# Moving the preparation transposes of a hybrid decoder kernel: both groups behind the up unit

## What is computed

```python
def swiglu_ffn(h, w_in, w_out):
    gate, up = jnp.split(h @ w_in, 2, axis=-1)
    return (jax.nn.silu(gate) * up) @ w_out

# S5, per group of 16 channels a 64-dimensional complex diagonal state
b_bar = ((lam_bar - 1.0) / lam)[:, :, None] * lax.complex(b_re, b_im)
bu = jnp.einsum('gph,btgh->btgp', b_bar, u_blk)
_, s = lax.associative_scan(_linear_recurrence_op, (a_elems, bu), axis=1)
y_blk = jnp.einsum('ghp,btgp->btgh', c, s).real
```

## Time and profile before

| | |
|---|---|
| median of 3 runs | 1010.5 us (1010.32 to 1010.53) |
| the profiled execution | 1009.69 us |
| its span | 1008.0 us |
| busy PE, DVE, ACT, POOL | 98%, 73%, 56%, 11% of the span |
| mean granted clock of PE | 0.998 |
| turns 7 to 21 in the span | 69.0 us to 212 us |

### The profile page before, as it was taken

How to read it: one execution, slowest core, us unless ns; L and a number is a source line. 1 busy time by engine, 2 the same in 40 slices (tenths; PEclk the granted TensorE clock), 3 DMA queues, 4 the chain that set the end, 5 groups by cost and what they waited for, 6 DMA issues and landing times.

```text
span 1008.0 us, 20116 instructions
## 1 busy us (share of the span) xinstructions
PE 990.0 (98%) x7672; PEld 923.4 (92%) x7672; DVE 738.5 (73%) x900; ACT 567.3 (56%) x790; POOL 111.6 (11%) x143
## 2 busy tenths in 40 slices
PE   8999999899899999999999999999999999999997
PEld 8999999899899999999999999999899898888886
DVE  5789885799976766666687666668566587666666
ACT  7444446583365655555565555555599765555555
POOL 4863138000001000000010000001000010000000
PEclk9999999999999999999999999999999999999999
DMA  8655554343065555555546556554643246556552
GB/s 253 191 181 173 172 173 159 130 151 119 23 210 188 173 193 182 187 185 188 185 147 210 187 187 187 187 187 148 219 137 127 84 147 211 192 192 189 189 188 110
DMA packets 49037, 172.42 MB, mean 171 GB/s; under 512 B 6096, under 2 KB 6096, under 8 KB 48976
## 3 DMA queue, kind: packets, MB, share of 16 engines
q1 hardware_dynamic: 48544, 170.99, 51.9%
q10 hardware_dynamic: 432, 0.55, 0.2%
HBM read 170.47 MB, written 1.05 MB: 170 GB/s over the span
## 4 chain that ended last, share of the span: by engine, by line
PE 74%; DVE 12%; POOL 6%; issue 4%; ACT 3%; DMA 1%; ACTq 0%; DVEq 0%; POOLq 0%; SPq 0%
PE mx L1195 11%; PE gu L1195 10%; PE mx L1198 6%; PE gu L1198 5%; PE gu L1180 5%; PE gu L1181 5%; PE gu L1182 5%; PE acc L1180 5%; PE acc L1181 5%; PE acc L1182 5%; DVE w_lo L732 3%; PE acc L1224 2%; PE acc L1226 2%; PE acc L1228 2%; ACT w_hi L334 1%
## 5 line engine op out<-in xcount | busy, mean ns | idle before, releaser
L804 DVE TENSOR_TENSOR w_lo<-raw,w_hi 128x1024 fp32r<-128x1024 f32 x178 | 217.2, 1222 | 56.2 <-ACT w_hi L419 55.2
L732 DVE TENSOR_TENSOR w_lo<-raw,w_hi 128x1024 fp32r<-128x1024 f32 x138 | 177.0, 1297 | 41.6 <-ACT w_hi L334 41.0
L419 ACT ACTIVATE w_hi<-raw 128x1024 fp32r<-128x1024 f32 x171 | 179.8, 1053 | 41.3 <-PE mx L1198 18.3
L1180 PE MATMUL gu<-g,w_hi 128*128 128x256 f32 x624 | 179.6, 288 | 1.9 <-DVE g L824 1.6
L1181 PE MATMUL gu<-g,w_hi 128*128 128x256 f32 x624 | 176.5, 283 | 0.0
L1182 PE MATMUL gu<-g,w_lo 128*128 128x256 f32 x624 | 176.4, 283 | 0.0
L334 ACT ACTIVATE w_hi<-raw 128x1024 fp32r<-128x1024 f32 x145 | 150.2, 1051 | 41.1 <-DMA raw<-wstream_dram 20.4
L1180 PE MATMUL acc<-h_hi,w_hi 128*128 128x256 f32 x504 | 143.6, 285 | 0.1
L1182 PE MATMUL acc<-h_hi,w_lo 128*128 128x256 f32 x504 | 142.6, 283 | 0.0
L1181 PE MATMUL acc<-h_lo,w_hi 128*128 128x256 f32 x504 | 142.6, 283 | 0.0
L1180 PEld LDWEIGHTS gu<-g,w_hi 128*128 128x128 f32 x624 | 119.5, 192 | 2.9 <-DVE w_lo L1099 2.1
(11 more groups left out here) (280 smaller groups left out, 1691.0 us busy)
## 6 DMA issues: line engine op xcount, KB each, us to landing
raw<-wstream_dram SPq DMA_DIRECT2D x318, 512.0 KB, 3.6
x<-x_in_dram SPq DMA_DIRECT2D x4, 256.0 KB, 5.7
raw<-wstream_dram SPq DMA_DIRECT2D x3, 256.0 KB, 5.7
out_dram<-x_tok SPq DMA_DIRECT2D x3, 256.0 KB, 2.0
gain_row<-last_gain_dram SPq DMA_DIRECT2D x1, 512.0 KB, 4.7
raw<-wstream_dram ACTq DMA_DIRECT2D x1, 256.0 KB, 4.3
s_memory<-b_re_dram SPq DMA_DIRECT2D x1, 256.0 KB, 4.5
s_memory<-b_im_dram SPq DMA_DIRECT2D x1, 256.0 KB, 4.6
```

Source lines behind the costliest of these rows:

```text
L419: act.activation(w_hi[:, n0 % RING, :], raw[:, n0 % RAW, :], ACT.Copy).then_inc(hi_ready, 1)
L732: dve.tensor_tensor(lo, raw[:, n % RAW, :], hi.bitcast(F32), ALU.subtract).then_inc(lo_ready, 1)
L804: dve.tensor_tensor(w_lo[:, n0 % RING, :], raw[:, n0 % RAW, :], w_hi[:, n0 % RING, :].bitcast(F32), ALU.subtract).then_inc(lo_ready, 1)
L1180: pe.matmul(dst, a, hi, start=start, stop=False, skip_group_check=check)
```

## The change

In the eight turns with transposes, PE no longer does the first of the turn's two groups between the gate unit and the up unit: both groups stand behind the up unit, one after the other. ACT reads both groups behind the rounding of the hidden block and ahead of the split of unit g0 + 6, where it read the first one behind the split of unit g0 + 4 and the second one behind the rounding. In turn 21, whose groups are 14 and 15, the reading of group 14 moves from the head of ACT's turn to the place behind the split of unit g0 + 4. The writing of `rho` in turn 20 now comes ahead of the reading of group 12. No instruction is added or taken away.

```diff
@@ scalar engine, prep_turn
                 if f == NF - 1:
-                    read_turned(late)
                     silu(0, f)
                     round_h(0, f)
                     split_after(g0)
+                    read_turned(late)
                     read_turned(late + 1)
                     split_after(g0 + 1)
                     return
                 split_after(g0)
-                if 0 <= early < 8:
-                    read_turned(early)
-                if 8 <= late < 16:
-                    read_turned(late)
                 if late == 12:
...
                 if 0 <= early < 8:
+                    read_turned(early)
                     read_turned(early + 1)
                 if 8 <= late < 16:
+                    read_turned(late)
                     read_turned(late + 1)
                 split_after(g0 + 2)
@@ tensor engine, prep_turn
                 column_unit(gu[:, f % 2, 0:SEQ], g0 % RING)
-                if 0 <= early < 8:
-                    turn(early)
-                if 8 <= late < 16:
-                    turn(late)
...
                 column_unit(gu[:, f % 2, SEQ:2 * SEQ], (g0 + 1) % RING)
                 if 0 <= early < 8:
+                    turn(early)
                     turn(early + 1)
                 if 8 <= late < 16:
+                    turn(late)
                     turn(late + 1)
```

## The result

| | before | changed |
|---|---|---|
| median, range | 1010.5 us, 1008.85 to 1012.43 (20 executions) | 1012.63 us, 1012.14 to 1013.61 (20 executions) |
| ratio, 95% interval | | 1.0023, 1.0016 to 1.0029 |
| the profiled execution, its span | 1009.69, 1008.0 us | 1012.33, 1010.6 us |
| fourth padding, group 9, squares | 141.74, 183.25, 223.77 us | 142.46, 183.93, 226.37 us |
| from the squares to the end of the span | 784.2 us | 784.2 us |

A forecast was written before the change was run, and what follows sets the result against it. Up to 183 us losses of DVE and ACT count, from there to the squares PE's, or DVE's beyond its slack. Terms 0.96 + 1.77 = 2.73 us on the 1010.5 median gave 1013.2 us; range 1011.4 to 1014.3.

The forecast's parts named there:

- PE's own work: PE's transposes move but none goes; two groups in series save nothing: 0 taken, bounds 0 to -0.24 us.
- First term: Turns 7 to 10: the added ACT reading delays DVE's wait for the split: +0.96 us, between 0.79 and 1.44.
- The stop in turn 12: PE's down unit waits for DVE's delayed low part of block 11: 0.4 to 0.5 us, within the 0.96.
- Second term: Turns 18 to 21: added readings delay DVE and ACT up to the squares: +1.77 us, 1.3 to 1.8.
- So there is no slack: At the squares, 223.77 us: DVE's last addition ends 0.10 earlier, where PE's series ends too.
- The new stop in turn 21: PE waits 1.1 us ahead of group 14, down unit about 1.2 late; counted at nothing, cover 0.5 us.
- The sum: Whole kernel: 0.96 + 1.77 = 2.73 us more, median 1013.2 us.
- absorbed: Rival: idle ACT swallows its delays and PE gains the second start, -0.24 us: 1010.3; chance 0.08.
- One stretch only: Rival: one of the two terms falls out, through unseen slack or faster DVE: 1011.5 or 1012.3; chance 0.20.
- The new stop adds: Rival: PE's later tail holds back DVE's norm, adding the 1.2 us stop on top: 1014.4; chance 0.10.

The follow-up runs named there:

- e1: Kernel before with only PE's order changed (both groups behind the up unit), ACT's order as before: 1010.48 us, ratio 1.0002.
- e4: Kernel before with the change in turns 18 to 21 only: 1011.25 us, ratio 1.0014.
- e7: Kernel before with ACT reading the third row of the kernels' second half ahead of the rounding in turn 17: 1008.07 us, ratio 0.9974.
- e11: Kernel before, unchanged, run and profiled again: 1010.5 us, ratio 1.0004.
- e9: Changed kernel, run and profiled again: 1012.6 us, ratio 1.0022 against before.
- e2: Kernel before with only ACT's order changed (both readings behind the rounding), PE's order as before: 1016.8 us, ratio 1.0063.
- e3: Kernel before with the change in turns 7 to 10 only: 1011.79 us, ratio 1.0013.
- e6: Kernel before with the second reading of turns 7 to 10 moved behind the first split of the next turn: 1010.41 us, ratio 0.9992.
- e5: Changed kernel with both readings moved behind the first split of the next turn: 1010.7 us, ratio 1.0001 against before.
- e8: Kernel before with the edits of e6 and e7 together: 1008.01 us, ratio 0.9982.
- e10: Changed kernel with the third row read ahead of the rounding in turn 17, as in e7: 1010.64 us, ratio 1.0007 against before.

## Why the prediction held, and where it was off

- **PE's own work, 0**: right (e1). Eight transposes in series put the second matmul behind them at 75.72 in turn 7 of the changed kernel, 0.87 us late, where twice 0.44 was forecast.
- **First term, turns 7 to 10**: the mechanism was right, turn by turn. The size was 0.96, "from the run that I have". Against that run 0.72 was measured, and 0.80 when both paddings are counted from the row at 81.5: the 0.79 that was worked out for a load that is prompt in the changed kernel. But the late load was an accident of one profile: e1, e4, e7 and e11 have no such load, and against e11 the padding of e9 is 1.40 us later (1.41 from that row), near the upper bound of 1.44. The step that failed is the load of 6.61 us taken as typical, and as late again in the changed kernel; its effect on DVE was priced rightly.
- **The stop in turn 12**: PE's down unit starts at 121.73, 0.36 us later than in a series with the matmul before it at 121.25, and its second matmul 0.44 later (121.93). 0.4 to 0.5 was forecast, as part of the first term.
- **Second term, turns 18 to 21**: forecast 1.77, measured 42.44 - 40.52 = 1.92 at a full clock in before. Of the 0.15 more, the first reading behind the rounding accounts for 0.13: in turn 18 of the changed kernel and of e9 it starts 0.45 us behind it (190.69 to 191.14 in e9), while the one reading there in before started 0.32 behind (189.82 to 190.14), as those of turn 10 do. I had priced each reading at 0.48 without that. The waits of DVE say the same: 0.93 in turn 19 as forecast, 1.07 in turn 18. Against before with a fallen clock, e11, the term is only 42.42 - 42.02 = 0.40. That is the step that fails for the median: "So there is no slack". With a fallen clock PE reaches the squares 1.5 us later, and most of DVE's delay hides behind that; I had taken the full clock of the one profile for granted.
- **The new stop in turn 21**: forecast 1.1 to 1.2 us and covered by 0.5. e9 has 1.14, and PE's last matmul ahead of the squares starts at 225.92 and so could be followed at 226.04, 0.50 ahead of the squares. Right, as was the distance to the end of the span.
- **The sum**: 2.73 was made of two terms against a profile that is neither of the two usual ones. Against e11 it is 1.40 + 0.40 = 1.80 at the squares, and 1012.58 - 1010.71 = 1.87 in time; against an execution with prompt load and full clock it is 1.40 + 1.92 = 3.3, and the fastest of both kernels are 1012.14 - 1008.85 = 3.3 apart. The median of before lies near the first kind and the medians are 2.1 apart, since a third of its executions are of the faster kind. So 1013.2 was 0.6 too high, and the 2.1 is at the lower edge of the forecast's 2.1 to 3.3. That it landed so near is in part luck: the first term was 0.44 too small, the second 1.37 too large for the usual execution, and neither the spread of the load nor the clock was among the rivals.
- **The rivals**: absorbed is out by e2 and e3. "One stretch only" had 1012.3 near the result, but both stretches cost (e3, e4). "The new stop adds" is out by e9. The rule of the Trainium skill, Perfetto Trace Analysis, Optimizing Tensor Performance, would have made the stop the cost: the stop is real, 1.14 us in e9, and worth nothing here. The rule of the Trainium skill, Perfetto Trace Analysis, Identifying the Most-Contended Engine, to go by the highest occupancy, would have left ACT out of sight: 56% busy, it is part of the loop that set the time.

## What to carry to other kernels

An engine that is idle half the time can still sit in a loop of releases. Ask of every moved instruction who waits for the one behind it, not how busy the engine is: 0.48 us of reading cost 0.48 in each turn in which DVE waited for the split, and nothing where it didn't. Taking out the reading that stood there before gave 0.1 to 0.2 us, since the next limit was close.

A stop of the bounding engine may have a second price. Look at several executions and their clocks before one profile's rows are added up: a difference of 1.5 us between executions of one kernel was as large as each term, and which kernel hides it decides part of the verdict. Where an edit shortens such a stop (e7), it may win more than the time cut from the stop.

## What the hardware showed unexpectedly

- The granted clock fell to 0.51 (the 1.2 GHz level) for some 3.3 us behind stops of PE of 2.57 to 2.61 us, starting 1.0 to 1.4 us behind the stop's end: in the changed kernel, e4, e6 and e11, and not in before, e1, e2, e3, e5 and e9, which had the same stop. In e2 it fell behind the 2.58 us stop of turn 21 instead, within 0.2 us of its end, and stayed at 0.50 for some 3 us. In e11 it costs 1.5 us of PE time (42.02 against 40.52). Behind the 1.49 us stop of e7, e8 and e10 it didn't fall in their profiles. The Trainium skill, TensorE: Matmul & The Clock Gate, Part 1: The HAM clock gate, says that the clock follows how busy PE has been recently, and of the slow start of a kernel that it varies from run to run; a fall behind some of these stops goes with both. What decides between fall and no fall behind equal stops is left open here.
- A load of 512 KB landed after 6.61 us in one profile of before and was not late in e1, e4, e7 and e11, which have the same readings in those turns; that one load shifted the padding by 0.5 to 0.7 us.
- At the start of e4 the mean clock of the first 15 us was 0.89 instead of 1.00, which moved the whole execution by 0.8 us.
